# Second expert layer: gather from the residual rows instead of a normalized copy, whose place is used for weights and sums

## What is computed

```
def hier_moe(h, w_group, b_group, w_router, b_router, w_gate, w_up, w_down):
    # h is rms_norm(residual, m_norm[layer]); 32 experts in 4 groups of 8, 2 chosen per token
    ...
    combine = ...                       # (tokens, 32): weight of each expert for each token, 0 if not chosen
    for e in range(N_EXPERTS):
        hid = silu(hf @ w_gate[e]) * (hf @ w_up[e])        # 1024 -> 256
        y = y + (hid @ w_down[e]) * combine[:, e:e + 1]    # 256 -> 1024

x = x + hier_moe(rms_norm(x, m_norm[layer]), ...)
rms_norm(x, g) = x * rsqrt(mean(x * x) + 1e-6) * g
```

## Time and profile before

| | |
|---|---|
| Median of three runs | 775.05 us (773.02 to 776.62) |
| Profiled execution | 774.8 us, span 773.1 us |
| TensorE (PE) busy | 720.5 us, 93% |
| its weight loads (PEld) | 459.7 us, 59% |
| VectorE (DVE) | 324.6 us, 42% |
| ScalarE (ACT) | 206.5 us, 27% |
| DMA | 241.62 MB, mean 313 GB/s |
| In the chain that ended last | PE 58%, DMA 12% |

### The profile page before, as it was taken

How to read it: one execution, slowest core, us unless ns; L and a number is a source line. 1 busy time by engine, 2 the same in 40 slices (tenths; PEclk the granted TensorE clock), 3 DMA queues, 4 the chain that set the end, 5 groups by cost and what they waited for, 6 DMA issues and landing times.

```text
span 773.1 us, 16718 instructions
## 1 busy us (share of the span) xinstructions
PE 720.5 (93%) x7450; PEld 459.7 (59%) x7450; DVE 324.6 (42%) x687; ACT 206.5 (27%) x415; POOL 31.5 (4%) x99
## 2 busy tenths in 40 slices
PE   8999999999989999899999999999998997787696
PEld 6778887648645564545647745785765553343342
DVE  7476886624363322343237054643345231221222
ACT  2574568316100000000033263540420100000004
POOL 7006000000000000000000000000000000000000
PEclk9999999999999998899999999999999998998899
DMA  8644113399999999999999814538789999999994
GB/s 259 211 93 157 57 57 112 125 416 419 385 421 418 422 420 420 419 422 420 414 350 350 279 54 167 199 139 342 287 327 421 417 422 418 421 421 423 420 403 176
DMA packets 75381, 241.62 MB, mean 313 GB/s; under 512 B 10078, under 2 KB 41948, under 8 KB 55724
## 3 DMA queue, kind: packets, MB, share of 16 engines
q1 hardware_dynamic: 75084, 240.00, 80.1%
q10 hardware_dynamic: 224, 0.54, 0.2%
HBM read 239.48 MB, written 1.05 MB: 311 GB/s over the span
## 4 chain that ended last, share of the span: by engine, by line
PE 58%; DMA 12%; DVE 4%; SPq 4%; issue 1%; ACT 0%; PEld 0%; PEldq 0%; ACTq 0%
PE ps L1605 11%; PE ps L1934 10%; PE ps L1434 7%; DMA M<-in_m_w_gate_dram 7%; PE ps L1536 7%; DMA M<-in_m_w_down_dram 5%; PE ps L1551 5%; PE ps L1690 4%; SPq L493 2%; DVE H L2550 1%; SPq L487 1%; PE ps L1079 1%; PE ps L1450 1%; PE ps L1828 1%; PE ps L1470 1%
## 5 line engine op out<-in xcount | busy, mean ns | idle before, releaser
L1605 PE MATMUL ps<-M 128*32 128x256 f32 x2008 | 124.0, 396 | 14.1 <-DMA M<-in_m_w_gate_dram 6.9
L1605 PEld LDWEIGHTS ps<-M 128*32 128x32 f32 x2008 | 66.2, 114 | 69.2 <-issue 15.9
L1133 PE MATMUL ps<-M 128*128 128x272 f32 x352 | 85.3, 397 | 0.3 <-DMA M<-in_e_w_in_dram 0.3
L1934 PE MATMUL ps<-M 128*128 128x256 f32 (+2 forms) x288 | 79.9, 434 | 0.0
L1536 PEld LDWEIGHTS ps<-M 128*128 128x128 f32 x608 | 71.6, 192 | 12.2 <-issue 11.8
L1536 PE MATMUL ps<-M 128*128 128x128 f32 x608 | 77.1, 279 | 0.0
L1133 PEld LDWEIGHTS ps<-M 128*128 128x128 f32 x352 | 65.6, 190 | 15.7 <-issue 1.7
L1690 PE MATMUL ps<-M 128*32 128x512 f32 x448 | 59.9, 682 | 11.8 <-DMA M<-in_m_w_down_dram 11.8
L1551 PE MATMUL ps<-M 128*128 128x512 f32 (+1 forms) x120 | 62.8, 647 | 5.4 <-DVE H L2550 5.4
L1934 PEld LDWEIGHTS ps<-M 128*128 128x128 f32 x288 | 53.7, 190 | 22.6 <-issue 15.6
L2547 DVE TENSOR_TENSOR H<-H,ps 128x512 f32<-128x512 f32 x60 | 41.3, 688 | 51.2 <-PE ps L1551 51.0
(11 more groups left out here) (473 smaller groups left out, 843.1 us busy)
## 6 DMA issues: line engine op xcount, KB each, us to landing
M<-in_m_w_gate_dram SPq DMA_DIRECT2D x28, 2048.0 KB, 18.3
M<-in_m_w_up_dram SPq DMA_DIRECT2D x22, 2048.0 KB, 21.3
M<-in_m_w_down_dram SPq DMA_DIRECT2D x20, 2048.0 KB, 21.1
M<-in_m_w_down_dram SPq DMA_DIRECT2D x15, 1024.0 KB, 17.4
M<-in_o_w_in_dram SPq DMA_DIRECT2D x12, 1024.0 KB, 9.4
M<-in_e_w_in_dram SPq DMA_DIRECT2D x11, 1024.0 KB, 5.8
M<-in_m_w_up_dram SPq DMA_DIRECT2D x10, 1024.0 KB, 17.1
M<-in_m_w_gate_dram SPq DMA_DIRECT2D x9, 1024.0 KB, 6.6
```

Source lines behind the costliest of these rows:

```text
L1133: ins = pe.matmul(ps[:, n % 4, 0:T], wringE[:, (n // 2) % 4, k, (n % 2) * P:(n % 2) * P + P], (xnE if n else xuE)[:, k], start=(k == 0), s ...
L1605: ins = pe.matmul(ps[32 * e:32 * e + 32, 3 * x, 0:FF], xgT[q % 2][:, k, 32 * e:32 * e + 32], w, start=(k == 0), stop=(k == KD - 1))
L1934: ins = pe.matmul(ps[rows, unit % 4, 0:n], lhs(k), rhs(k), start=(k == 0), stop=(k == KD - 1))
```

## The change

In the second layer (`y` = 1) only:

- The copy `xn` isn't written. The gathers take `H[:, n, k::KD]` itself as the stationary operand (`tokens`), 128 floats that lie 8 floats apart. Layer 0 still uses `xn`.
- So the reciprocal root has to come in elsewhere: the one-hot rows are first written as 0 and 1 into `RW`, and then multiplied by `rs` into `R` (`scaled_onehot`), a second VectorE instruction behind a wait. `weighted` then reads `RW` and overwrites it. The overflow loop does the same in its own form.
- The 8 KB per partition that `xn` took (columns 24576 to 26623 of `M`) now first hold `up` of expert 0 (`up0`), loaded when `mix_part` is 4. `slots[1][:, 0]`, which held it, gets `down` 4 instead, at the old time; what `down` 4 took of the later loads falls away.
- `H` must stay as it is until the last gather, so the experts' sums go to `total`, which takes the same place when `up0` has been used. The first sum reads `H` and writes `total`. The last group, the final norm and the output read `total`.
- Scratch rows for the squares of the final norm lie in `yst[0]` (`junkY`).

```diff
+        total = at(24576, 2, D)
+        up0 = at(24576, 2 * D)
...
-                            sp.dma_start(slots[1][:, 0, :], up[:, 0, :]).then_inc(s("ld_s1"), 16)
+                            sp.dma_start(slots[1][:, 0, :], down[:, 4, :]).then_inc(s("ld_lruw_e5"), 16)
...
                             sp.wait_ge(s("mix_part"), 4)
+                            sp.dma_start(up0, up[:, 0, :]).then_inc(s("ld_s1"), 16)
                             sp.dma_start(slots[2][:, 3, :], down[:, 3, :]).then_inc(s("ld_s2"), 16)
...
-                            sp.dma_start(slots[j][:, 0:2, D * h:D * h + D], src[:, 4:6, D * h:D * h + D]).then_inc(s(f"ld_s{j}"), 16)
+                            sp.dma_start(slots[j][:, 1, D * h:D * h + D], src[:, 5, D * h:D * h + D]).then_inc(s(f"ld_s{j}"), 16)
...
-                act.wait_ge(s("rec"), (5, 10)[y])
-                normed(0)
-                if nt == 3:
+                if y == 0:
+                    act.wait_ge(s("rec"), 5)
+                    normed(0)
                     normed(2)
...
+            def tokens(y, n, k):
+                return H[:, n, k::KD] if y else xn[:, n, k, :]
...
-                        ins = pe.matmul(ps[:, GATHER_BANK[k // 2], (k % 2) * P:(k % 2) * P + P], xn[:, n, k, :], R[:, n, :],
+                        ins = pe.matmul(ps[:, GATHER_BANK[k // 2], (k % 2) * P:(k % 2) * P + P], tokens(y, n, k), R[:, n, :],
...
-                            ins = pe.matmul(ps[:, 1 + k // 4, (k % 4) * P:(k % 4) * P + P], xn[:, n, k, :], R[:, n, :],
+                            ins = pe.matmul(ps[:, 1 + k // 4, (k % 4) * P:(k % 4) * P + P], tokens(y, n, k), R[:, n, :],
...
-                pe.wait_ge(s("xn_set"), (3, 5)[y])
+                if y == 0:
+                    pe.wait_ge(s("xn_set"), 3)
...
+                    ins = tt((RW[0] if y else R)[:, t_].rearrange("p t (e c) -> p t e c", e=4),
+                             iota[:, 1:CAP + 1].unsqueeze(1).unsqueeze(1).to_broadcast([P, m, 4, CAP]),
+                             RM[:, t_, 0:4].unsqueeze(3).to_broadcast([P, m, 4, CAP]), ALU.is_equal)
+                    if y:
+                        link(ins)
+                        ins = scaled_onehot(0, t_, m)
+                    return ins.then_inc(s("R_set"), 1)
+
+                def scaled_onehot(q, t_, m):
+                    return tt(R[:, t_], RW[q % 2][:, t_], rs[:, ri, t_].unsqueeze(2).to_broadcast([P, m, P]), ALU.mult)
...
-                def accumulate(j):
+                def accumulate(j, first=False):
...
-                        return tt(H[:, n, c], H[:, n, c], ps[:, 6 + j % 2, :], ALU.add)
+                        return tt((total if y else H)[:, n, c], (total if y and not first else H)[:, n, c], ps[:, 6 + j % 2, :], ALU.add)
```

More of the change, by code:

```diff
@@ L586, in first_part @@
                 cnt = TILES[n][1]
-                link(nc.scalar.activation(tmp[0:cnt, n, 0:512], H[0:cnt, n, 0:512], ACT.Square, accum_out=ss[0:cnt, i, n:n + 1]))
+                src = H if i < 4 else total
+                link(nc.scalar.activation(tmp[0:cnt, n, 0:512], src[0:cnt, n, 0:512], ACT.Square, accum_out=ss[0:cnt, i, n:n + 1]))
                 link(nc.scalar.activation(ss[0:cnt, i, n:n + 1], ss[0:cnt, i, n:n + 1], ACT.Identity, bias=epsb[0:cnt, 0:1], scale=1.0 / D))
@@ L907, in experts @@
                     act.wait_ge(s("acc"), a0 + i + 1)
-                    first_part(2 + 2 * y, n, junkT)
+                    first_part(2 + 2 * y, n, junkY if y else junkT)
                 if y == 0:
@@ L1510, in last_rows @@
                 logits(1, range(6, 8)).then_inc(s("lg_done"), 1)
-                pe.wait_ge(s("xn_set"), (2, 4)[y])
+                if y == 0:
+                    pe.wait_ge(s("xn_set"), 2)
                 pe.wait_ge(s("R_set"), (NQ + 1) * y + 1)
@@ L1602, in half_gu @@
                                 w = apart[e][:, FF * k:FF * k + FF]
+                            elif u == 1 and y == 1 and e == 0:
+                                w = up0[:, FF * k:FF * k + FF]
                             elif u == 1 and y == 1 and e >= 2:
@@ L1646, in experts @@
                             for t in range(2):
-                                pe.matmul(ps[:, 1 + t, :], ident[:, :], H[:, t, 512:D], start=True, stop=False)
+                                pe.matmul(ps[:, 1 + t, :], ident[:, :], total[:, t, 512:D], start=True, stop=False)
                             pe.wait_ge(s("ld_half"), 176)
@@ L2625, in experts @@
                                 assert n_step[0] == OVSTEPS
-                                tt(R[:, t_, 0:CAP], iota[:, 0:CAP].unsqueeze(1).to_broadcast([P, nt, CAP]), wide3(rme, CAP), ALU.is_equal) \
-                                    .then_inc(s("ov_R"), 1)
-                                v.wait_ge(s("ov_R"), i)
-                                tt(RW[1][:, t_, 0:CAP], R[:, t_, 0:CAP], wide3(wte, CAP), ALU.mult).then_inc(s("ov_RW"), 1)
+                                if y == 0:
+                                    tt(R[:, t_, 0:CAP], iota[:, 0:CAP].unsqueeze(1).to_broadcast([P, nt, CAP]), wide3(rme, CAP), ALU.is_equal) \
+                                        .then_inc(s("ov_R"), 1)
+                                    v.wait_ge(s("ov_R"), i)
+                                    tt(RW[1][:, t_, 0:CAP], R[:, t_, 0:CAP], wide3(wte, CAP), ALU.mult).then_inc(s("ov_RW"), 1)
+                                else:
+                                    for t in range(2):
+                                        ins = stt(out=R[:, t, 0:CAP], in0=iota[:, 0:CAP], scalar=rme[:, t:t + 1],
+                                                  in1=rs[:, ri, t:t + 1].to_broadcast([P, CAP]), op0=ALU.is_equal, op1=ALU.mult)
+                                    ins.then_inc(s("ov_R"), 1)
+                                    for t in range(2):
+                                        ins = stt(out=RW[1][:, t, 0:CAP], in0=iota[:, 0:CAP], scalar=rme[:, t:t + 1],
+                                                  in1=wte[:, t:t + 1].to_broadcast([P, CAP]), op0=ALU.is_equal, op1=ALU.mult)
+                                    ins.then_inc(s("ov_RW"), 1)
                                 v.wait_ge(s("ov_g"), i)
@@ L2654, in last_accumulate @@
                         c = slice(512 * hf, 512 * hf + 512)
-                        ins = tt(H[:, t, c], H[:, t, c], ps[:, bank, :], ALU.add)
+                        x = total if y else H
+                        ins = tt(x[:, t, c], x[:, t, c], ps[:, bank, :], ALU.add)
                     else:
@@ L2671, in experts @@
                         v.wait_ge(s("acc"), at0 + t + 1)
-                        tt(fin[:, t, 0:512], H[:, t, 0:512], fnb[:, 0:512], ALU.mult).then_inc(s("fin_set"), 1)
+                        tt(fin[:, t, 0:512], total[:, t, 0:512], fnb[:, 0:512], ALU.mult).then_inc(s("fin_set"), 1)
                 if y == 0:
```

29 lines of the change are left out of this document (16 added, 13 removed).

## The result

The changed kernel takes 783.6 us (median of 6 runs, 779.81 to 787.45), the kernel before, timed beside it, 775.88 us (6 runs, 773.02 to 776.62): ratio 1.0113, interval 1.0093 to 1.0132. By this ratio it is slower by 8.8 us, with an uncertainty of 1.5 us; the two medians differ by 7.7 us. Forecast were 781.4 us, 6.6 us more than before, and "slower by over 0.5%" as the likeliest case; the direction and the mechanism held, the size was 1 to 2 us short.

A forecast was written before the change was run, and what follows sets the result against it. The end of the weight stream, one FIFO with gaps, was taken to bound the kernel. 774.8 + 5.3 (late issue for q = 4) + 1.3 (tail) = 781.4 us; range 771.9 to 786.

The forecast's parts named there:

- one-number model of the stream: Weight loads form one FIFO; its end moves with the bytes left at its last gap and the length of its gaps.
- Part 1: One expert's 1 MiB load moves to an earlier gap at 530.1 us: -2.5 us, delaying nothing and opening no hole.
- Part 2: The copy leaves ScalarE, two copies of 2.16 us that TensorE did not wait for: gain nothing.
- Part 3: VectorE writes one-hot rows twice: +0.6 us in the routing chain before 566.6 us, +0.45 us at group q = 2.
- Part 4: Layer 1's gather loads become strided, 32 bytes apart: 116 ns extra per load, bounds 0 and 140 ns.
- the two readings: For strided loads: each fresh stretch of memory costs, or stepping costs 0.9 ns a column whatever the step, so nothing is lost.
- rival A: The stride is free for a f32 load; only parts 1 and 3 remain, 772.9 us; chance 0.25.
- The delay of the issue for q = 4: Gate weights issued at 629.12 us come 14.7 us later: 120 strided loads at 0.116 plus 0.3 and 0.45; reserve 9.4 us.
- The stream, +5.3: After the late q = 4 issue the weight stream begins again at 646.6 instead of 641.3 us, 5.3 us later.
- the tail, +1.3: Last gather: 16 strided loads behind the last down weights but one, +1.9 us, less TensorE's reserve of 0.58 us.
- C: A price in between, 83 ns extra per load: 776.8 us, no change; chance 0.10.
- D: The new 1 MiB collides with the load of 545.97; later loads 2.5 us late, 775.4 with free strides; with others 0.07.

The follow-up runs named there:

- complement pair: The changed kernel, strided only in the gathers for q = 5 to 7: ratio 1.0007; strided only up to the gather for q = 4: ratio 1.0134.
- step series: The changed kernel with steps of 1, 2, 3, 4, 5, 6, 8, 16 floats, one per k, in layer 1's later gathers: one execution, 779.22 us.

## Why the prediction was right, and where it was off

**What bounds the kernel, and the one-number model of the stream.** Right. The dry stretches, the last weights and the chain follow from "delay of an issue less its reserve", and the complement pair shows it most clearly: 1.0007 with the stride only where there is reserve, 1.0134 with it only where the reserve isn't enough.

**Part 1, -2.5 us and no new hole.** Right that it doesn't count once the stream is late (1.0119 without it, 1.0113 with it). Wrong that no hole opens: with contiguous gathers one of some 1.5 us stands at 574 to 577 us. What the move is worth while the stream is not late was not run by itself. Two kernels with doubled rows and contiguous gathers bracket it: 0.9999 with the move (and without the copy), 1.0028 without it. That is 2.2 us in its favour with an uncertainty of 2.3, so the gain of about 1 us that the hole leaves is neither shown nor excluded.

**Part 2, nothing.** Right within what the times can tell: with the copy still there, 1.0118, without it 1.0113.

**Part 3, +0.6 and +0.45 us.** The first term was measured as 0.64 us. The second wasn't found in the profile: the issue for q = 4 is no later than before. The timing asks for more than both, 0.4 to 4.0 us. Why is open. One thing can be said about it: the one profile of the kernel before ends slowly. Without its filler it differs in nothing that counts (1.0007), and yet its aligned span is 1.15 us shorter than that of the kernel before. Aligned differences against the kernel before may therefore be about 1 us too small. For the changed kernel that would fit the ratio (7.7 us aligned, 8.8 timed), but the medians differ by 7.7 themselves. For the doubled rows the gap is larger: aligned, that kernel ends 0.5 us before the kernel before (773.6 - 1.03 - 773.1), timed it is 2.2 us slower, and at most 1.15 of these 2.7 us would be explained so.

**Part 4, 116 ns a load.** The mechanism was right, the price a little low. From the chain of waits of the changed kernel, in the same view as the 1.98 us in the earlier trace rows:

```profile
591.61 4.01 PE ps L1546 x16
```

(4.01 - 1.98) / 16 = 127 ns, against 116 forecast and inside the bounds of 0 and 140. The upper bound was worked out wrongly: 1.9 to 2.1 ns a column over 128 columns are 243 to 270 ns, not 225 to 247, so it should have been 270 + 17 - 124 = 163 ns, and the range would have reached some 3 us higher. The measured value lies within either. The recorded duration of a load is 333 ns where some 310 was to show it. The choice between the two readings rested on ScalarE's 2.16 us for the same pattern, and this was the argument that carried. The one from the 198 ns did not.

The Trainium skill says (SBUF — State Buffer, Specifications (TRN2)) that lines have 16 bytes and that two hits on each are enough for full bandwidth. The step series agrees with it in detail: 192 ns at 4 hits, 196 at 2, 312 to 334 at 1. The prediction's remark that two hits already cost 58 ns was the mistake, not the rule. The Trainium skill's rule that a load takes its columns divided by 1.2 (TensorE: Matmul & The Clock Gate, LDWEIGHTS), which was rival A, agrees here with the pace of contiguous loads (107 ns) and not with that of the strided ones, 127 ns dearer.

**The delay of the issue for q = 4: 14.7 us predicted, 16.3 measured.** The gate matmuls behind the first gather were to start near 567.5 us and did so at 569.1; the difference is the filler (3.45 - 1.88 = 1.57 us), and it is the whole difference at q = 4 too: 16.3 - 1.6 = 14.7. The kernel with a filler of 1.88 us and the stride alone is 13.5 us late. That the sum without the filler agrees to 0.1 us is partly luck: with 127 ns for 116 it would be 16.0, so about 10 of the 120 loads must hide somewhere; with the stride alone 13.5 / 0.127 gives 106 of 120 that show. Where they hide isn't shown. What the sum lacked is the fall of the granted clock: it was named as a danger ("if the longer loads make the granted clock fall") and given no price, and it measured 1.6 us at this issue. The longer loads are also not its cause by themselves: with the stride alone the filler kept its 1.88 us, and a kernel with contiguous loads at this place lost the clock too (2.27 us).

**The stream, +5.3, measured 6.5; the tail, +1.3, measured 1.2.** 16.3 - 9.4 = 6.9 was to be expected from the measured delay. At the issue for q = 1 the delay is 7.4 us (5.9 forecast, 591.67 - 4.90 against 579.39), less the reserve of 3.1 a smaller hole, which the later one contains. The tail came as worked out; TensorE, not the last weights, now sets it.

**Rivals.** A (free stride, 772.9) and C (a price in between, 776.8) are excluded by 333 ns and by the time. D, a collision of the new megabyte with the load at 546, is seen at a small size and didn't reach the end: that load lands 9.0 us after its issue in the changed kernel and 9.1 in the one with contiguous gathers, 7.8 before and 7.6 with the megabyte taken back. So "delays nothing" in part 1 was wrong by some 1.3 us. The price that D forecast without the stride, 775.4, isn't excluded by the 774.26 (0.9999, up to 1.0018) of the contiguous gathers alone; what speaks against it is that the dry stretches at 556 and 566 us, which can absorb the delay, are still there.

## What to carry to other kernels

Before a copy is dropped because its engine is idle, ask which reader the layout was made for: here ScalarE spent 4.3 us off the path, so that TensorE saved 127 ns on each of 256 loads. A weight stream has a reserve at each issue, and an edit costs the largest of delay less reserve over all issues, so the changed kernel is 1.3% slower with slow loads in the first five gathers only, and not slower (1.0007) with them in the last three only. Fillers that were free inside a wait stand on the path as soon as the work before them grows, so look at them first when such a stage gets longer.

## What the runs showed of the hardware

- A load of 128 f32 columns takes 192 ns contiguous, 196 with a step of 8 bytes, 261 with 12, and 312 to 334 from 16 to 64 bytes.
- At the lower level of the granted clock a load of contiguous columns takes 333 ns, as long as one with a step of 32 bytes (338), whose duration hardly depends on the clock (335 at the full one). The first 12 matmuls of the gather show it: first the kernel that is strided only for q = 5 to 7, contiguous here, then the step series, strided here:

```profile
L1459 PEld LDWEIGHTS ps<-M,H x12: 263/333/337, 560.8 to 563.1; 128*128 128x128 f32 x12
560.70:563.60 2.90, 2.81 (x13) 2.82 (x14) 2.52 (x14) 0.46 (x2) 0.00 (x0) 0.53 0.98 374
```

```profile
L1459 PEld LDWEIGHTS ps<-M,H x12: 313/338/338, 560.4 to 563.0; 128*128 128x128 f32 x12
560.30:563.50 3.20, 3.10 (x13) 3.10 (x14) 2.74 (x15) 0.60 (x3) 0.00 (x0) 0.52 1.00 369
```

At a granted clock of 1.00 the contiguous block takes 1.60 us and the strided one 3.09, at 0.53 and 0.52 they take 2.90 and 3.24. So in these blocks a fall of the clock costs the contiguous gather 1.3 us and the strided one 0.15, and the filler behind it, which has no stride, pays in full.

- Weights in pieces of 1 KB move at 350 GB/s, in whole pieces of 8 KB at 420.
- The granted clock fell for a few us around the first gather in some kernels and not in others. The filler there, 4 matmuls, takes 1.88 us at the full clock. In the profiles it took 1.88 in the kernel before and with the stride alone (no added wait in front), and, with the added wait of 0.4 us, 1.88, 1.88, 1.88, 2.08, 2.27, 2.28, 2.77, 3.04, 3.45 and 3.55 us. Three kernels with the wait and the filler kept the full clock, so did the one with the wait and no filler (1.00), and one with contiguous loads here lost it (2.27). So neither the wait nor the stride decides alone; what does is open. One profile for each kernel can't tell it from scatter.
